# Reciprocal standard deviation of three layer norms as one GpSimd power in place of a ScalarE root and a VectorE reciprocal

## The reference, cut to what matters

```python
def layer_norm(x, g, b):
    mu = jnp.mean(xf, axis=-1, keepdims=True)
    var = jnp.mean(jnp.square(xf - mu), axis=-1, keepdims=True)
    return ((xf - mu) * lax.rsqrt(var + LN_EPS) * g + b)
...
h = layer_norm(x, ln_in_g, ln_in_b)
for l in range(DEPTH):                      # DEPTH = 2
    y = token_mixer(h, ...)
    h = layer_norm(DEEPNORM_ALPHA * h + y, ln1_g[l], ln1_b[l])
    f = swiglu(h, ...) if l % 2 == 0 else moe_ffn(h, ...)   # layer 0 dense, layer 1: 8 experts
    h = layer_norm(DEEPNORM_ALPHA * h + f, ln2_g[l], ln2_b[l])
```

## Time and profile before

| | |
|---|---|
| median of 3 runs | 1997.81 us (1990.95 to 2000.44) |
| profiled execution, its own time | 2005.28 us |
| its span in the trace | 2003.6 us |
| TensorE matmul busy | 1926.7 us (96%) |
| VectorE busy | 1434.1 us (72%) |
| ScalarE busy | 1127.7 us (56%) |
| GpSimd busy | 99.6 us (5%) |
| mean granted TensorE clock | 0.981 |

### The profile page before, as it was taken

How to read it: one execution, slowest core, us unless ns; L and a number is a source line. 1 busy time by engine, 2 the same in 40 slices (tenths; PEclk the granted TensorE clock), 3 DMA queues, 4 the chain that set the end, 5 groups by cost and what they waited for, 6 DMA issues and landing times. The chain is left out here.

```text
span 2003.6 us, 27175 instructions
## 1 busy us (share of the span) xinstructions
PE 1926.7 (96%) x11117; PEld 1664.5 (83%) x11117; DVE 1434.1 (72%) x1600; ACT 1127.7 (56%) x1240; POOL 99.6 (5%) x160
## 2 busy tenths in 40 slices
PE   6998999999999989989999999999999999999995
PEld 5797989899987879988888888888888888888884
DVE  4876356644337674375797988879889798897996
ACT  2355343444333544343776766767767677676773
POOL 5003000100021011001000000000000000000000
PEclk9998999999999999999999999999999999999998
DMA  6222246455432232183699999999999999999992
GB/s 170 81 74 88 64 119 208 126 168 169 149 77 64 64 98 85 43 242 106 230 372 310 368 352 322 377 318 354 358 318 372 328 348 369 307 372 334 341 370 108
DMA packets 260485, 456.98 MB, mean 228 GB/s; under 512 B 32218, under 2 KB 111274, under 8 KB 260356
## 3 DMA queue, kind: packets, MB, share of 16 engines
q1 hardware_dynamic: 258966, 454.74, 66.3%
q10 hardware_dynamic: 1390, 0.44, 0.1%
HBM read 452.11 MB, written 3.04 MB: 227 GB/s over the span
## 5 line engine op out<-in xcount | busy, mean ns | idle before, releaser
L390 DVE TENSOR_TENSOR wl<-ring,wh 128x2048 fp32r<-128x2048 f32 x385 | 880.3, 2289 | 244.9 <-ACT wh L384 241.8
L384 ACT ACTIVATE wh<-ring 128x2048 fp32r<-128x2048 f32 x385 | 739.6, 1923 | 317.9 <-PE ps L359 317.8
L359 PE MATMUL ps<-wh,xgh 128*128 128x512 f32 x896 | 354.4, 396 | 2.4 <-DVE wl L390 2.4
L359 PE MATMUL ps<-wh,xgl 128*128 128x512 f32 x896 | 349.4, 390 | 0.0
L359 PE MATMUL ps<-wl,xgh 128*128 128x512 f32 x896 | 349.1, 390 | 0.0
L359 PE MATMUL ps<-hPh,ringr 128*128 128x288 f32 x1024 | 237.3, 313 | 10.5 <-DVE ringr L441 6.9
L359 PEld LDWEIGHTS ps<-wh,xgh 128*128 128x128 f32 x896 | 168.3, 188 | 39.9 <-DVE wl L390 5.8
L359 PEld LDWEIGHTS ps<-wh,xgl 128*128 128x128 f32 x896 | 168.2, 188 | 35.8
L359 PEld LDWEIGHTS ps<-wl,xgh 128*128 128x128 f32 x896 | 168.5, 188 | 33.1
L359 PEld LDWEIGHTS ps<-hPh,ringr 128*128 128x128 f32 x1024 | 177.2, 196 | 16.9 <-issue 9.6
L359 PE MATMUL ps<-hPl,ringr 128*128 128x288 f32 x512 | 155.8, 304 | 0.0
(11 more groups left out here) (416 smaller groups left out, 2818.6 us busy)
## 6 DMA issues: line engine op xcount, KB each, us to landing
ring<-in_moe_w SPq DMA_DIRECT2D x336, 1024.0 KB, 5.6
ring<-in_w_in SPq DMA_DIRECT2D x38, 1024.0 KB, 5.2
ring<-in_ffn_w SPq DMA_DIRECT2D x33, 1024.0 KB, 5.3
ring<-in_w_out SPq DMA_DIRECT2D x8, 1024.0 KB, 8.2
ring<-in_w_in SPq DMA_DIRECT2D x32, 128.0 KB, 3.3
ring<-in_w_oa SPq DMA_DIRECT2D x16, 256.0 KB, 4.9
ring<-in_w_ob SPq DMA_DIRECT2D x8, 512.0 KB, 7.2
resid<-in_x_prompt SPq DMA_DIRECT2D x1, 1024.0 KB, 5.1
```

Source lines behind the costliest of these rows:

```text
L359: ins = nc.tensor.matmul(*a, **k)
L384: nc.scalar.activation(wh[:, k % WS, :], ring[:, s:s + SLOT], ACT.Copy).then_inc(hi_ready, 1)
L390: ins = nc.vector.tensor_tensor(wl[:, k % WS, :], ring[:, s:s + SLOT], wh[:, k % WS, :].bitcast(F32), ALU.subtract)
```

## The change

The root and its table loads are gone from ScalarE, and the reciprocal from VectorE. VectorE adds the small constant to the variance by an instruction of its own, and GpSimd raises the result to the power of minus one half by an element-wise operation whose second operand is a column of -0.5 that is read 288 times. GpSimd does that first, and then subtracts the mean, now from the last five tiles (3 to 7). VectorE subtracts it from the first three, between its addition and its wait for the power.

```diff
-        eps = sb("eps", [P, 2])
+        root = sb("root", [P, 2])[:, 0:1]
...
-            c(nc.gpsimd.memset(eps[:, 0:1], LN_EPS))
-            c(nc.gpsimd.memset(eps[:, 1:2], 4 * LN_EPS))
+            c(nc.gpsimd.memset(root, -0.5))
...
-        EPS = [1, 0, 1]
+        EPS = [4 * LN_EPS, LN_EPS, 4 * LN_EPS]
...
-            act.wait_ge(nvar_ready, q + 1)
-            nc.scalar.activation(sdev, var, ACT.Sqrt, bias=eps[:, EPS[q]:EPS[q] + 1]).then_inc(nstd_ready, 1)
...
         def centred(pool, q):
 
+            pool.wait_ge(nvar_ready, q + 1)
+            nc.gpsimd.tensor_tensor(rsd, var, root.to_broadcast([P, T]), ALU.pow).then_inc(nstd_ready, 1)
             pool.wait_ge(nst_ready, 2 * q + 2)
-            for k in range(XC_POOL):
+            for k in range(KD - XC_POOL, KD):
                 nc.gpsimd.tensor_tensor(hT[:, k, :], hT[:, k, :], mean, ALU.subtract).then_inc(xc_ready, 1)
 
         def normalised(dve, c, q):
 
             Q = SUMB[q][1]
             dve.wait_ge(nst_ready, 2 * q + 1)
-            nc.vector.scalar_tensor_tensor(out=var, in0=ps[Q][:, 0:T], scalar=1.0 / D, in1=msq, op0=ALU.mult, op1=ALU.subtract
-                                           ).then_inc(nvar_ready, 1)
+            c.link(nc.vector.scalar_tensor_tensor(out=var, in0=ps[Q][:, 0:T], scalar=1.0 / D, in1=msq, op0=ALU.mult, op1=ALU.subtract))
+            nc.vector.tensor_scalar(var, var, EPS[q], None, ALU.add).then_inc(nvar_ready, 1)
+            dve.wait_ge(nst_ready, 2 * q + 2)
+            for k in range(KD - XC_POOL):
+                ins = nc.vector.tensor_tensor(hT[:, k, :], hT[:, k, :], mean, ALU.subtract)
+            c.link(ins)
             dve.wait_ge(nstd_ready, q + 1)
-            c.link(nc.vector.reciprocal(rsd, sdev))
             for k in range(KD):
-                if k < XC_POOL:
-                    dve.wait_ge(xc_ready, XC_POOL * q + k + 1)
-                else:
-                    c.link(nc.vector.tensor_tensor(hT[:, k, :], hT[:, k, :], mean, ALU.subtract))
+                if k >= KD - XC_POOL:
+                    dve.wait_ge(xc_ready, XC_POOL * q + k - KD + XC_POOL + 1)
                 nc.vector.tensor_tensor(tn[:, k, :], hT[:, k, :], rsd, ALU.mult).then_inc(tn_ready, 1)
...
-                        if j == N_MERGE - AHEAD:
-                            nc.scalar.activation(std[:, 0:1], std[:, 0:1], ACT.Sqrt)
...
-                    nc.scalar.activation(std[:, 0:1], std[:, 0:1], ACT.Sqrt)
```

More of the change, by code:

```diff
@@ L163, in program @@
         sqx = [tn[:, m, :] for m in range(2)]
-        msq, var, sdev = tn[:, 2, :], tn[:, 3, :], tn[:, 4, :]
+        msq, var = tn[:, 2, :], tn[:, 3, :]
         mean, rsd = work[:, KD * T:KD * T + T], work[:, KD * T + T:KD * T + 2 * T]
```

## The result

The changed kernel takes 2132.89 us (2131.2 to 2135.55, 4 runs) against 1996.37 for the kernel before: 136.5 us more, ratio 1.0679 (95% interval 1.0662 to 1.0696). It lies far above the forecast of 2015 and its range. The page of the changed kernel shows the place at once.

What follows compares the result with a forecast made beforehand. TensorE was taken to bound the kernel. Tile delays 12.9, less 0.6 won back, plus 5.2 for the clock gave +17.5 us on the median 1997.8, so 2015; range from 1994 less 2 to 2042.

Steps and rivals of the forecast that it cites:

- The place of the price: In each of three norms (q = 0, 1, 2), the power delays the tiles that TensorE waits for.
- P: Time of one power on GpSimd in each norm, estimated at 6.8 us.
- P - 2.1: Delay of the norm's first tile, which decides at q = 0 and q = 2: 4.7 us each.
- P - 3.3: Delay of the norm's last tile, which decides at q = 1: 3.5 us.
- Upper end: Highest price for the power on GpSimd: about twenty assumed steps, each as dear as a subtraction, 15.8 us.
- very dear: Rival: the power on GpSimd takes over 16 us; at 30 us the kernel takes 2086 us; chance 0.17.
- The clock: TensorE at half clock after its longer waits: 2.2 us at q = 0 and q = 1, 0.8 at q = 2, together 5.2.
- VectorE's subtractions under P: VectorE's three subtractions, about 0.45 us each, fit beside GpSimd's power if that takes over 1.4 us.
- that rival: Cheap power on GpSimd, 0.8 to 4.8 us: kernel time 1994 to 2001 us in its examples, within 0.5%; chance 0.38.
- Table loads at nothing: Four ScalarE table loads of 1.28 us go; hidden by other waits, they win nothing, at most 4 x 1.5 us uncovered.
- 7.5: Microseconds taken off three times the power's time to give the tile delays of the three norms together.
- 0.6: Microseconds won back at q = 0, where TensorE waited 0.58 for a low part that VectorE now finishes earlier.

Runs made afterwards that it cites:

- power_warm57: The changed kernel with 57 unread products in place of 5 at the head of the three blocks: 2132.21 us against 2132.89.
- root_back: The changed kernel with ScalarE's root, preloaded tables and VectorE's reciprocal in place of the power, new split of subtractions kept: 2006.9 us, ratio 1.0038 to the kernel before.
- apart: As root_back, but GpSimd's subtractions start only when VectorE's three are done: 2003.81 us, ratio 1.0026 to the kernel before.
- power_half: The changed kernel with the power on 144 of 288 columns, the rest by ScalarE's root and VectorE's reciprocal: 2065.53 us, ratio 1.033 to the kernel before.

## Why the prediction was wrong, point by point

**The place of the price was right.** The power stands on the chain, first tile at q = 0 and 2, last tile at q = 1. It starts 0.88 us after the variance does (0.94 forecast). The first tile was to be later by P - 2.1; with the measured P = 46.4 that is 44.3, and TensorE's idle grew from 0.40 to 45.06, by 44.7. At q = 1 the last tile was to be later by P - 3.3 = 43.1. The stretch grew by 41.9, but that is no confirmation, as it scatters by 4. The rows of the last multiplication and of TensorE's first run of products say more:

```profile
628.86 0.46 DVE L723 SCALAR_TENSOR_TENSOR resid<-ps,resid 128x288 f32<-128x288 f32 x1 [3.16 <-ACT resid L701]
...
676.08 4.65 POOL L717 TENSOR_TENSOR hT<-hT,resid 128x288 f32<-128x288 f32 x5
...
681.89 0.44 DVE L733 TENSOR_TENSOR resid<-hT,resid 128x288 f32<-128x288 f32 x1
```

The last multiplication starts 53.03 after the variance, against 8.30 before: 44.7 later. GpSimd has subtracted from its last tile by 680.73; the forecast put the last multiplication 0.03 after that, and it comes 1.16 after, as VectorE is behind. TensorE's first run of products ends 59.05 after the variance, against 14.07: 45.0 later.

**The step that failed is P.** "A power is two, a logarithm and an exponential, so P = 6.8 is my value": it is 46.4, 6.8 times as much. "Upper end: ... it would be 20 x 0.79 = 15.8" was no upper end either. Both were scaled from GpSimd's subtraction, 0.79 us for 288 columns or 2.75 ns a column. The power takes 160 ns a column, nearly 59 subtractions' worth. Nothing in the trace of before bounded it from above, and I took an assumed number of steps for a bound. The rival "very dear" named the kind, but at P = 30, with 0.17, and the range left it out. What I held against it, that GpSimd's other operations are all near one pass, was misread: one of them in the trace of before, a multiplication, took 3.57 us for 128 columns, 28 ns a column, ten times the subtraction's.

```profile
L1646 POOL TENSOR_TENSOR arena<-arena,cT 128x128 f32<-128x128 f32 x2 | 7.1, 3570 | 0.0
```

That row doesn't price a power, but it shows that the price of one subtraction bounds nothing. The Trainium skill, page "GPSIMD Engine Reference", section "3. Performance versus the Vector engine", puts element-wise work at about twice VectorE's price, and the page says so of ordinary arithmetic. Twice the reciprocal's 1.95 would have been an estimate of 3.9 for the power, further off than mine; the measured 46.4 decides. Why a column takes 160 ns stays open; that it is the same for 1 and for 128 partitions says that partitions are served side by side, and that it grows in step with the columns says that columns aren't.

**The clock was mis-sized.** 5.2 us were put down for it; the run with the clock kept up at q = 0 and q = 1 won 2.5 in the stretches and 0.7 in the medians, neither clear of scatter. The stretches of half clock were there as forecast, about 6 us at q = 0. But at q = 0 a part of what TensorE loses in them it would otherwise wait for VectorE's low parts (0.82 us in power_warm57), and at q = 1 the first four tiles come only every 0.97 us.

**VectorE's subtractions under P: right, but a cost beside it was left out.** They fit under the power, 1.66 us. But the sum took VectorE's element-wise work as independent of GpSimd's. Eight multiplications take 5.97 us in the change, beside GpSimd's five subtractions, against 3.04 in root_back, where GpSimd has finished. That is why the last multiplication at q = 1 is over a microsecond behind GpSimd's last tile. The trace of before already had a multiplication of 1.04 us beside 0.46 for the median (the row of L733 above). Beside P = 46.4 this is nothing. No run has a cheap power, so what it would have made of that rival isn't shown; root_back, 0.4% slower than before without any power, says only that the new split of the subtractions isn't free.

**Table loads at nothing: not contradicted.** They are gone from the change, and the stretches show no gain that asks for one. Taking P as measured, the forecast's own terms give 3 x 46.4 - 7.5 - 0.6 = 131.1 without the clock, against 133.4 in the stretches. The 2.3 between them is less than one stretch scatters by; the clock and VectorE's hold-up both lie in it and aren't told apart.

## What to carry to other kernels

An operation that no row of the trace shows has no upper bound from the rows of other operations; its price should be measured off the path first, which one run of a probe in an idle stretch does. Before work is moved to an idle engine, ask not how idle it is (GpSimd stood at 5%) but what a single instruction takes when it is waited for: three instructions of 46 us cost this kernel 134. And VectorE and GpSimd at element-wise work with two inputs at once aren't two engines' worth: VectorE's instructions of that kind took over twice their time beside GpSimd's subtractions, and GpSimd's waited out VectorE's large ones. Last, a difference in one stretch of one trace is to be set beside what that stretch does between kernels that are the same there, before it is read as a gain.

## What the runs showed of the hardware that I had not expected

- GpSimd's element-wise power of fp32: 46.4 us for 288 columns, 23.5 for 144, 15.8 for 96, 8.0 for 48, 0.70 for 2; for 96 columns the same within 5% on 1, 16 and 128 partitions and for exponents -0.5, 1.0 and 2.0.
- VectorE's 128x288 subtraction beside a GpSimd subtraction: three in 3.02 us, against 1.19 when GpSimd waits. GpSimd loses less there, five in 4.45 against 4.01. VectorE's reciprocal, with one input, isn't held up: 1.95 us in apart, wholly beside GpSimd's subtractions, and 1.95 in root_back, where they end 0.58 us before it does.
- Beside a large two-input instruction of VectorE (128x2048, 2.29 us) it is GpSimd that loses: a 128x288 multiplication took 2.75 us against 0.67 to 0.81 for subtractions of that size just before, and a low part in root_back 4.53 us against 0.8 to 1.0, ending 0.65 after VectorE's instruction did.
- VectorE isn't held up throughout by the power. Its three subtractions beside it took 1.66 us in the change (1.42 in power_half), against 1.19 when alone.
